# Between blocks: residual additions and squares follow each scaling on VectorE, and the next projection's first two units run together, k-step by k-step

## The reference, cut to what matters

```python
def _rms_norm(x, g):
    xf = x.astype(jnp.float32)
    y = xf * lax.rsqrt(jnp.mean(xf * xf, axis=-1, keepdims=True) + RMS_EPS)
    return (y * g.astype(jnp.float32)).astype(x.dtype)
...
    for layer in range(DEPTH):              # DEPTH = 2
        h = _rms_norm(x, norm_mix_pre[layer])
        m = _even_mixer(h, ...)             # layer 1: _odd_mixer
        x = x + _rms_norm(m, norm_mix_post[layer])
        h = _rms_norm(x, norm_ffn_pre[layer])
        f = _conv_ffn(h, ...)               # first step: h @ w_up
        x = x + _rms_norm(f, norm_ffn_post[layer])
```

## Time and profile before

| | us |
|---|---|
| median of 3 runs | 2330.51 |
| lowest and highest run | 2329.67, 2344.09 |
| profiled execution, its own time | 2343.45 |
| its span | 2341.7 |

### The profile page before, as it was taken

The page is one execution under the profiler, slowest core; times in us unless marked ns, Lnnn a source line. Parts: engine busy times, 40 slices in busy tenths (PEclk is TensorE's granted clock), DMA queues, the critical chain, the costliest instruction groups (busy, mean ns, idle before and its releaser), DMA issues.

```text
span 2341.7 us, 28300 instructions
## 1 busy us (share of the span) xinstructions
PE 2202.6 (94%) x10835; PEld 1818.3 (78%) x10835; DVE 1221.1 (52%) x1795; ACT 802.6 (34%) x1185; POOL 129.4 (6%) x78
## 2 busy tenths in 40 slices
PE   7988898999998997789999998999899999999998
PEld 6855576888886894677888886878888998888887
DVE  5344627643556437556634557762766325642542
ACT  4244534333334216543333334453211113221322
POOL 1000003000003001021000003000100000000000
PEclk9978998999998998899999998998999759999999
DMA  4100021323222220012223222221000002222221
GB/s 165 65 29 37 18 72 54 107 81 102 105 69 94 96 102 6 19 54 90 94 85 108 94 86 84 105 84 63 1 1 1 19 1 73 90 95 103 90 93 69
DMA packets 24717, 164.04 MB, mean 70 GB/s; under 512 B 2736, under 2 KB 2864, under 8 KB 8368
## 3 DMA queue, kind: packets, MB, share of 16 engines
q1 hardware_dynamic: 24048, 161.29, 19.6%
q10 hardware_dynamic: 576, 1.46, 0.2%
HBM read 160.65 MB, written 2.10 MB: 69 GB/s over the span
## 4 chain that ended last, share of the span: by engine, by line
PE 87%; DVE 5%; POOL 4%; ACT 2%; issue 1%; DMA 0%; SPq 0%; ACTq 0%; DVEq 0%; POOLq 0%
PE bank L278 22%; PE bank L280 22%; PE bank L279 22%; PE bank L422 2%; POOL x L1628 2%; POOL y L1628 2%; PE bank L690 2%; PE bank L679 2%; PE bank L436 2%; PE bank L398 2%; PE bank L689 1%; PE bank L450 1%; PE bank L730 1%; PE bank L719 1%; PE bank L724 1%
## 5 line engine op out<-in xcount | busy, mean ns | idle before, releaser
L278 PE MATMUL bank<-hH,wH 128*128 128x512 f32 x1584 | 627.5, 396 | 28.8 <-DVE hL L1174 20.4
L279 PE MATMUL bank<-hL,wH 128*128 128x512 f32 x1584 | 622.8, 393 | 0.0
L280 PE MATMUL bank<-hH,wL 128*128 128x512 f32 x1584 | 622.5, 393 | 0.0
L1140 DVE TENSOR_TENSOR wL<-raw,wH 128x2048 fp32r<-128x2048 f32 x160 | 371.1, 2319 | 284.1 <-ACT wH L759 284.0
L278 PEld LDWEIGHTS bank<-hH,wH 128*128 128x128 f32 x1584 | 301.6, 190 | 96.9 <-issue 24.4
L759 ACT ACTIVATE wH<-raw 128x2048 fp32r<-128x2048 f32 x160 | 304.9, 1905 | 189.7 <-PE bank L280 186.0
L280 PEld LDWEIGHTS bank<-hH,wL 128*128 128x128 f32 x1584 | 301.1, 190 | 63.9
L279 PEld LDWEIGHTS bank<-hL,wH 128*128 128x128 f32 x1584 | 301.5, 190 | 62.2
L279 PE MATMUL bank<-mL,wH 128*128 128x512 f32 x608 | 236.5, 389 | 0.0
L278 PE MATMUL bank<-mH,wH 128*128 128x512 f32 x608 | 236.5, 389 | 0.0
L280 PE MATMUL bank<-mH,wL 128*128 128x512 f32 x608 | 236.5, 389 | 0.0
(11 more groups left out here) (292 smaller groups left out, 2888.2 us busy)
## 6 DMA issues: line engine op xcount, KB each, us to landing
raw<-in_ffn_up SPq DMA_DIRECT2D x44, 1024.0 KB, 4.8
raw<-in_mlp_up SPq DMA_DIRECT2D x16, 1024.0 KB, 4.8
raw<-in_mlp_down SPq DMA_DIRECT2D x16, 1024.0 KB, 4.8
raw<-in_ffn_down SPq DMA_DIRECT2D x16, 768.0 KB, 4.4
raw<-in_dn_qkv SPq DMA_DIRECT2D x12, 1024.0 KB, 4.8
raw<-in_ffn_down SPq DMA_DIRECT2D x16, 640.0 KB, 3.9
raw<-in_even_in SPq DMA_DIRECT2D x9, 1024.0 KB, 5.0
raw<-in_even_out SPq DMA_DIRECT2D x4, 1024.0 KB, 4.9
```

What stands on the lines that cost most here:

```text
L278: mm(out, a, c, start=first, stop=False)
L279: mm(out, a, d, start=False, stop=False)
L280: return mm(out, b, c, start=False, stop=last)
L1140: tt(wL[s][:], raw[s][:], wH[s][:].bitcast(F32), ALU.subtract).then_inc(w_split, 1)
```

## The change

In `post_pre`, VectorE adds all eight tiles to `x`, each behind its own scaling, with `lo_pre` one tile behind instead of three, and with `wL` of unit 1 (`lo_early(name)`) moved from behind `u7` to between `u1` and `x2`. All seven additions of squares are VectorE's, in one chain behind `u7`. GpSimd's additions at the four junctions are gone (12 instructions at each). On TensorE the new `first_two_units` replaces `first_unit` and the following unit: 0 and 1 are interleaved, and `token_sums` and `spread` stand in front of k-step 6 of unit 1's first and second tile. `mix_pre0` and `mlp2` keep the old way.

```diff
+            def first_two_units(tag, name):
+                def step(s, tl, k):
+                    c = slice(k * 256 + tl * P, k * 256 + tl * P + P)
+                    last = three(bank[2 * s + tl][:], (wH[s][:, c], wL[s][:, c]), (hH[:, k, :], hL[:, k, :]), k == 0, k == KT - 1)
+                    if k == KT - 1:
+                        last.then_inc(mm_done, 1)
+                def steps(s, k):
+                    for tl in range(2):
+                        step(s, tl, k)
+                for k in range(2):
+                    pe.wait_ge(*at(f"{tag}.u{k}"))
+                    steps(0, k)
+                pe.wait_ge(w_split, UNIT0[name] + 2)
+                for k in range(2):
+                    steps(1, k)
+                for k in range(2, 4):
+                    pe.wait_ge(*at(f"{tag}.u{k}"))
+                    steps(0, k)
+                    steps(1, k)
+                for k in range(4, KT):
+                    pe.wait_ge(*at(f"{tag}.u{k}"))
+                    steps(0, k)
+                for tl in range(2):
+                    for k in range(4, KT):
+                        if k == 6:
+                            if tl == 0:
+                                token_sums(tag, f"{tag}.ss")
+                            else:
+                                spread(tag)
+                        step(1, tl, k)
...
+            pairwise = ("ffn_pre0", "mix_pre1", "ffn_pre1", "mix2")
...
                         if first and peeled(i) and s == 0:
                             tile_wait(name, 1)
+                            if first in pairwise:
+                                tile_wait(name, 3)
+                                first_two_units(first, name)
+                                break
                             first_of(first)
                             continue
...
-                for k in range(KT + 3):
+                for k in range(KT + 1):
                     if k < KT:
                         stt(y[:, k, :], y[:, k, :], v(post, k), bank[6][:], ALU.mult, ALU.mult)\
                             .then_inc(*tick("norm_dve", f"{post}.t{k}"))
-                    if k == 1:
-                        dve.wait_ge(*at(f"{post}.t0"))
-                        tt(x[:, 0, :], x[:, 0, :], y[:, 0, :], ALU.add).then_inc(*tick("norm_dve", f"{post}.x0"))
-                    if k >= 3:
-                        lo_pre(tag, k - 3)
-                lo_early(name)
-                last_squares(tag)
+                    if k >= 1:
+                        lo_pre(tag, k - 1)
+                    if k == 2:
+                        lo_early(name)
+                    if k < KT:
+                        dve.wait_ge(*at(f"{post}.t{k}"))
+                        tt(x[:, k, :], x[:, k, :], y[:, k, :], ALU.add).then_inc(*tick("norm_dve", f"{post}.x{k}"))
+                dve.wait_ge(*at(f"{tag}.sq1"))
+                chain(tt(ss[:], y[:, 0, :], y[:, 1, :], ALU.add), "norm_dve", f"{tag}.squares1")
+                for k in range(2, KT):
+                    dve.wait_ge(*at(f"{tag}.sq{k}"))
+                    last = tt(ss[:], ss[:], y[:, k, :], ALU.add)
+                    if k < KT - 1:
+                        chain(last, "norm_dve", f"{tag}.squares{k}")
+                last.then_inc(*tick("norm_dve", f"{tag}.ss"))
                 inverse_kept(tag, name)
...
-            def add(tag):
-                for k in range(1, KT):
-                    pool.wait_ge(*at(f"{tag}.t{k}"))
-                    tt(x[:, k, :], x[:, k, :], y[:, k, :], ALU.add).then_inc(*tick("norm_pool", f"{tag}.x{k}"))
-            add("mix_post0")
-            first_squares("ffn_pre0")
-            add("ffn_post0")
-            first_squares("mix_pre1")
...
-            add("mix_post1")
-            first_squares("ffn_pre1")
-            add("ffn_post1")
-            first_squares("mix2")
```

## The result

| | before | after |
|---|---|---|
| median, us | 2342.05 (20 runs, 2328.48 to 2344.72) | 2349.04 (20 runs, 2342.59 to 2351.99) |
| ratio | | 1.0042, 95% interval 1.0027 to 1.0056 |
| profiled execution, us | 2343.45 | 2349.88 |

The change makes the kernel 0.42% slower, some 10 us (6 to 13), where the forecast was +6.5 us and "no difference". The three runs shown ahead of the prediction happened to hold two of the quick ones; over 20 runs the median of before is 2342, not 2331. The 2349 lies in the range given, but the difference is clear of the noise, and it is more than the sum said.

A forecast was written before the change was run, and what follows sets the result against it. The time of `ss`, through VectorE's and ScalarE's chain, was taken to set unit 3 at three of four junctions. +1.5 us over the junctions and +5.0 for the clock made +6.5: median 2330.51 to 2337, range 2324 to 2350.

The forecast's parts named there:

- `ss` and not TensorE sets unit 3: At three of four junctions, the time of `ss` sets unit 3's start as closely as TensorE's own work does.
- the +1.5 us: Sum over the four junctions without the clock: 1.2 lost, 0.9 gained, 0.2 gained, 1.4 lost.
- the price of `hL` without GpSimd: On VectorE at the junctions, `hL` (`u` in the prediction) takes 0.74 us once GpSimd is idle.
- 2.15 us a tile: VectorE's loop of `x`, ScalarE's `hi` and `u` costs 2.15 us per k-tile.
- `ss` 1.4 us later: At junction 1 `ss` comes at 382.2 instead of 380.84, 1.4 us later.
- 2 us at the sums: TensorE reaches `token_sums` at 380.3 at junction 1 and waits 2 us there for `ss`.
- The rival that `hL` keeps 1.36 us: At the junctions `hL` keeps its 1.36 us average, adding 19.5 us: 2356, slower by over 1%; chance 0.04.
- the one by which unit 3 does not wait for the chain: Case within the slightly-faster rival (chance 0.17): TensorE's own gains stand, 9.4 us, giving 2321.
- the term of the clock: Clock falls after waits in front of unit 3, 2.5 us each, at two of three junctions: +5.0 us, bounds 0 and 7.5.
- the 0.9 us of gain: Junction 2: `odd_q` has no such chain, so unit 2 starts 9.8 us after the old S instead of 10.7.
- the clock rival: The clock falls at every new wait, also at the sums of four junctions: +16 us, 2346; chance 0.20.
- S + 4.8: With 12 matmuls between sums and spread, the spread ends 4.8 us after the sums' start S.

The follow-up runs named there:

- fill_both: Kernel after plus unread matmuls, 13 before unit 3 at junctions 1, 3, 4 and 7 before the sums at all four; ratio to before 0.9997.
- squares_inside: Kernel after with only each square added inside VectorE's loop, sums and spread in front of k-step 4 instead of 6; ratio to before 0.9997.
- early_split: Kernel after with the splits of units 3 and 4 put before work on units 1's and 2's tiles at junctions 1, 3, 4; ratio to before 0.998.
- best1: Kernel after with early splits of units 3 and 4, and `odd_q`'s first tiles before the lambda computation at junction 2; ratio to before 0.9981.
- best2: Kernel after with early splits, `odd_q` tiles before lambda, squares inside VectorE's loop, sums before k-step 4; ratio to before 0.991 (six runs), repeated 0.9941.
- split_before: Kernel before with only the early split of units 3 and 4 added; ratio to before 0.9995.
- fill_unit3: Kernel after plus 13 unread matmuls in front of the wait for unit 3 at junctions 1, 3 and 4; ratio to before 1.0018.

## Why the prediction was wrong

**Right, step by step.** That `ss` and not TensorE sets unit 3, and the +1.5 us that follow from it (+1.3 in fill_both, where the clock is held up); the price of `hL` without GpSimd (0.75); 2.15 us a tile; `ss` 1.4 us later (1.5); no wait for unit 1's weights; 2 us at the sums (1.7 to 1.95); in front of unit 3 waits of 3.5 to 4.2 us (3.33, 3.32, 4.18); half clock behind them. The rival that `hL` keeps 1.36 us fell with the first profile, the one by which unit 3 does not wait for the chain as well.

**Wrong: the term of the clock.** The sum took a fall "at two of three" waits, 5.0 us. It came at all three, 1.8 + 3.2 + 2.3 = 7.3 us; filling the waits gave 5.5 back net, 7.0 without junction 2. And the sum left the clock behind the sums to a rival with a chance of 0.20, that is, put it at nothing, although junction 3 of the kernel before showed one behind a wait of 1.3 us. There it fell at junctions 1 and 2. At 1 it put unit 3 at +2.2 instead of +1.2, at 2 it ate the 0.9 us of gain. The 2.3 and the 1.9 us are what +6.5 lacked against the 10.4 of the table, less 0.4 that junctions 3 and 4 did better. The true case lies between the forecast and the clock rival (+16), which priced a fall at the sums at every junction at 1.7 us; it happened at two and cost about 1 at each. So the failed step is the term of the clock: 5.0 us in the sum, 9.2 us measured.

The Trainium skill (TensorE: Matmul & The Clock Gate, "HAM oscillation") was cited for waits that make each next burst start cold. For the three waits in front of unit 3 the trace agrees at every one, and so do seven more waits of 2.5 to 3.8 us in front of unit 3 or 5 in squares_inside, early_split, best1 and both profiles of best2: behind each the granted clock is 0.50 to 0.64 over the next 4 us. Why these fell and the 2.19 us in front of junction 2's unit 2 in fill_both did not (1.00) is not shown. I had weakened it by a row of the attention, where a stretch behind a 4.04 us wait shows 0.64; that row is no milder case, since a granted clock of 0.64 over 4 us is a fall inside the stretch: it is 1.00 from 943 to 944 us and 0.54, 0.50 and 0.50 in the three behind it.

**Slips without effect.** The 1.36 us of the earlier trace rows is the mean over forty `hL`, eight of them outside the junctions; at the junctions it is 1.43. And with 12 matmuls between the sums and the spread the spread ends at S + 4.6 by the prediction's own numbers, not S + 4.8.

**Wrong: what counts as no difference.** Within 1% the kernels are the same, as forecast, but twenty runs of each tell 0.15%, and by these the change is a loss. The forecast of +6.5 us (0.28%) should have been called one. The base was off too: 2330.51 was the median of three runs of a kernel whose runs reach from 2328 to 2345.

**What stays open.** Why the clock fell behind the sums at some junctions and not at others with the same wait: before it did at junction 3 only, after at 1 and 2, in split_before, whose edit stands behind the sums, at 2 and 3. In the seven kernels where TensorE waits 1.3 to 2 us for `ss` it fell at 11 of 28 junctions (the copy of the factor then comes 6.4 to 8.0 us behind the start of the sums instead of 5.4 to 5.5). In the four profiles where it waits less than 0.4 us or not at all there (fill_both, squares_inside, best2 twice) it fell at none of 16. That speaks for the wait as a condition; what decides between equal cases is not shown. Where the clock falls is read from one execution of each kernel; the timed runs show only the sum.

## What to carry to other kernels

When an engine's wait is taken away, look at what the next engine-to-engine chain was released by: if that event doesn't move, the time saved becomes a wait further on, here of 3.3 to 4.2 us. Put the preparation of the next operand (here the split of unit 3's weights) in front of work that nobody waits for yet, before or together with such a change. And give a new wait of TensorE of 3 to 4 us the price of a slow start, here 1.8 to 3.2 us, in the sum and not as a risk.

## What the runs showed of the hardware

VectorE's instructions with two operands in SBUF take longer while GpSimd adds: `hL` 1.43 us on average at a junction instead of 0.75, the split of 2048 columns 3.38 instead of 2.29, the first addition of squares 1.77 instead of 0.68. The scaling, whose second tensor comes from the PSUM bank, takes 0.74 in both. The groups of VectorE by form at junction 1 (355 to 384 us), two of before and one of after:

```profile
L1174 DVE SCALAR_TENSOR_TENSOR hL<-x,vec,hH 128x512 fp32r<-128x512 f32 x8 | 11.2, 1434 | 0.0
L1198 DVE TENSOR_TENSOR ss<-y 128x512 f32<-128x512 f32 x1 | 1.8, 1769 | 0.0
```

```profile
L1213 DVE SCALAR_TENSOR_TENSOR hL<-x,vec,hH 128x512 fp32r<-128x512 f32 x8 | 6.0, 752 | 1.7 <-ACT hH L798 0.8
```

This is what the Trainium skill says (SBUF — State Buffer, "Who interferes with whom": an instruction of VectorE with two SBUF inputs contends with a GpSimd instruction that reads SBUF), and the trace agrees.

Moving GpSimd's work over therefore costs far less than its own time: 12 additions of 0.69 us came, 8.3 us per junction, and VectorE's other work there became shorter by about 8 x 0.68 + 1.1 + 1.1 = 7.6 us. By the two pages VectorE is busy for 1221.1 us before and 1223.7 after, 2.6 us more at four junctions, while GpSimd lost 84.

Matmuls on data that nobody needs, thirteen in each of three waits and seven in each of four, made the kernel faster by 0.45% (1.0042 to 0.9997). I had expected the sign but not that it could be measured beside 2340 us.

Twenty runs of the kernel before reach from 2328 to 2345 us. In the eleven profiles what lies outside of the four stretches takes from 1927.4 (split_before) to 1947.8 us (fill_unit3). Part of it is the stretch with the scan. It has three lengths: 104.0 us at a granted clock of 0.65, 100.2 at 0.69 (best1, best2) and 94.7 at 0.72, and no other in any of the eleven.
